# Norm factors spread by a transpose, three layer-norm tiles added up ahead by GpSimd, and rope's sine products moved to the vector engine

## The chip, the cores and the metric

The kernel runs on one core of a Trainium2 chip. The metric is the device time of one execution in microseconds (us), the median of three runs.

## What is computed

Two decoder layers over 1024 positions and 1024 channels, everything in float32. Of the reference, what bears on the change:

```python
h = _rmsnorm(x, mix_norm_gain[layer])
q, k, v, conv_in = jnp.split(h @ w_in[layer], ...)
q = _rope(_rmsnorm(q, q_norm_gain[layer]), cos, sin)      # per head of 64: x1*cos - x2*sin, x2*cos + x1*sin
k = _rope(_rmsnorm(k, k_norm_gain[layer]), cos, sin)
attn = _dilated_attention(q, k, v)
a, g = jnp.split(conv_in, 2, axis=-1)
u = _causal_dwconv(a * jax.nn.sigmoid(g), ...)            # 31 taps, 512 channels
u = jax.nn.silu(_layernorm(u, ...))                       # over the 512 channels
x = x + jnp.concatenate([attn, u], -1) @ w_out[layer]
h = _rmsnorm(x, ffn_norm_gain[layer])
x = x + (silu(gate) * val of a 3-tap conv of h @ w_up) @ w_down[layer]
```

## The kernel before

Activations stand transposed in SBUF: channels on the 128 partitions, the 1024 positions along a row, so a tile is 128x1024. TensorE is written here as PE, the vector engine as DVE, ScalarE as ACT, GpSimd as POOL, the queue of the sync engine as SP.

**Order of the work.** Each engine has its program written out by hand, and semaphores that only count up tie them together; `at(l, per_layer, base, step, i)` is the count that a wait asks for in layer `l`, pass `i`. A layer has these stages:

1. Input projection: 20 units of 48 matmuls (8 k-tiles, 3 products of split operands, 2 halves of 512 columns), two PSUM buffers `mm`. They come in four groups of four: value and gate of one of four conv channel tiles (`CT = 4`), then the two halves of one of four query or key groups (`QKG = 4`); then four units for v. The loop `Fori(0, QKG - 1)` has the next group's units beside the last group's norm and rope.
2. Attention: 2 turns (`TURNS`) of 4 heads times 8 query blocks, 32 steps a turn. DVE's mask operation (L1085) reads PSUM `mm` and the table `logcount`, and between steps DVE runs the last conv taps (L1118), 22 a turn.
3. The sum over channels for the layer norm (L573), output projection `out_unit`, 8 units; then the FFN in 11 groups.

**What DVE does in the projection.** Beside each unit it splits the weights (`lo`, L931), multiplies the result by the norm factor (`scaled`, L943) and runs conv taps (`taps`, L964), each `y = u_pad * tap + y` over a whole tile with a drain behind it. In each group it also runs `qk_norm` (L998, L999) and `qk_rope`: o1 = ta*cos (L1006), o2 = tg*cos (L1007), a drain, then the wait for `qk_sin`, then o1 - m2 and o2 + m4 (L1012, L1013). m2 = tg*sin and m4 = ta*sin are POOL's (L1281, L1282), which start when DVE's drain at L1001 has counted `qk_normed` up. In the last group `read_v` sits between the wait and L1012: it reads a unit of v out of PSUM (L943). ACT then copies o1 and o2 into m2 and m4, SP stores them and loads the heads for attention from there.

**Spreading a factor.** The sum of squares of 128 positions is one number for each position. `sums` makes it (L421), POOL raises it to -1/2 (`rsqrt`, L1257), ACT repeats it 128 times along a row (`widen`), and `spread` (L430) turns it so that the factor lies along the positions, eight 128x128 blocks by the identity into `stat_b`. There are seven a layer: one for the first norm, four for query and key, one for the layer norm, one for the second norm.

**Layer norm mean.** The sum over 512 channels of y is made on PE by a matmul of `ones` with each of the four tiles of y, for two halves: eight matmuls (L573), behind attention's last operation. DVE subtracts the mean (L1144). POOL's other adds are `add_squares` (L1264), the squares of query and key (L1271) and the squares of the layer norm (L1285). The tiles ahead of a y tile are ready when its taps are: `conv_y` counts them, the second near the end of attention's first turn, the third in the middle of the second, the fourth near its end.

Of the kernel before, what the change touches and what calls it, by code (L numbers as in the profile page):

```python
# [26 lines left out]
ALU = mybir.AluOpType  # L27
# [3 lines left out]
P = 128  # L31
D_MODEL = 1024
SEQ = 1024
# [17 lines left out]
CT = CONV_CH // P  # L51
# [3 lines left out]
QKG = 2 * HEADS // HPT  # L55
# [19 lines left out]
QK_STORES = 16 * 4 * HPT * QKG  # L75
# [49 lines left out]
def trunk(nc, xT, positions, weights, gains, qk_gains, conv_par, ffn_par, inv_freq, mask, outT):  # L125
    ctx = ExitStack()
    with ctx:
        def sb(name, shape, dt=F32, to=ctx):
            return to.enter_context(nc.sbuf_tensor(name, shape, dt))

        def sem(name):
            return ctx.enter_context(nc.semaphore(name))
# [9 lines left out]
        sin = sb("sin", [P, SEQ])  # L142
        logcount = sb("logcount", [P, SEQ])
        rinv = sb("rinv", [P, SEQ])
        ident = sb("ident", [P, P])
        ones = sb("ones", [P, P])
# [14 lines left out]
        y = sb("y", [P, CT, SEQ], to=mixer)  # L161
        u_pad = sb("u_pad", [P, CT, TAPS - 1 + SEQ], to=mixer)
# [3 lines left out]
        m2 = sb("m2", [P, SEQ], to=proj); m4 = sb("m4", [P, SEQ], to=proj)  # L166
        o1 = sb("o1", [P, SEQ], to=proj); o2 = sb("o2", [P, SEQ], to=proj)
        tg = sb("tg", [P, SEQ], to=proj); ta = sb("ta", [P, SEQ], to=proj)
        sa = sb("sa", [P, SEQ], to=proj); sb_ = sb("sb_", [P, SEQ], to=proj)
        v_raw = (o1, ta, tg, ta)  # L170
        proj.close()
        attn = ExitStack()

# [24 lines left out]
        stat_b, stat_s = aux  # L198
# [28 lines left out]
        gate_pre = sem("gate_pre"); gate_sig = sem("gate_sig")  # L227
        conv_u = sem("conv_u"); conv_first = sem("conv_first"); conv_y = sem("conv_y")
        qk_copied = sem("qk_copied"); qk_sqsum = sem("qk_sqsum")
        qk_normed = sem("qk_normed"); qk_sin = sem("qk_sin"); qk_roped = sem("qk_roped")  # L230
        qk_hi = sem("qk_hi"); qk_lo = sem("qk_lo")
        qk_stored = sem("qk_stored")
        v_ready = sem("v_ready"); v_turn_full = sem("v_turn_full"); v_turned = sem("v_turned")
# [20 lines left out]
        def at(l, per_layer, base, step=0, i=0):  # L254

            return l * per_layer + i * step + base
# [12 lines left out]
        def plain(eng):  # L269


            eng.sem_inc(waits_passed, 1)
# [104 lines left out]
        def _(pe):  # L377
# [3 lines left out]
            for acc, src in ((mm[0], o1), (mm[1], o2)):  # L381
                for c in range(HPT):
                    last = pe.matmul(acc[:, c * quarter:(c + 1) * quarter], ta[:, c * P:(c + 1) * P],
                                     src[:, 0:quarter], start=True, stop=True)
# [15 lines left out]
            with pe.Fori(0, DEPTH) as l:  # L400
# [24 lines left out]
                def spread(wide, s0, b0, step=0, i=0):  # L425

                    pe.wait_ge(widened, at(l, SMALL, s0 + 1, step, i))
                    pe.wait_ge(statb_read, at(l, STAT_B, b0 + 1, step, i))
                    for b in range(TB):
                        last = pe.matmul(stat_b[:, b * P:(b + 1) * P], wide[:, b * P:(b + 1) * P], ident[:],  # L430
                                         start=True, stop=True)
                    last.then_inc(statb_full, 1)

                def norm_sums(squares, norm, s0):
# [8 lines left out]
                pe.wait_ge(down_read, at(l, DOWN, 2))  # L443
                norm_sums(squares1, 0, 0)
                unit(1, 1, 1, 1, midway=lambda: spread(sb_, 0, 0))
                unit(0, 0, U_QK, U_QK)
                unit(1, 1, U_QK + 1, U_QK + 1)
# [11 lines left out]
                sums((sa[:],), headsum[:], HPT, QKG)  # L459
                unit(1, 1, U_V + 1, U_V + 1)  # L460
                spread(sb_, QKG, QKG)

                def turn_v(t):
# [101 lines left out]


                pe.wait_ge(conv_y, at(l, CT, CT))
                for half in range(2):
                    cols = slice(half * BANK, (half + 1) * BANK)

                    pe.wait_ge(pt_read[half], at(l, TURNS * PT_TURN // 2, TURNS * PT_TURN // 2 + 1))
                    for c in range(CT):
                        last = pe.matmul(stat_b[:, cols], ones[:], y[:, c, cols], start=c == 0, stop=c == CT - 1)  # L573
                last.then_inc(statb_full, 1)
                pe.wait_ge(o_split, at(l, 2 * PAIRS, 2 * PAIRS))
                out_unit(0, 0)
# [302 lines left out]
        def _(dve):  # L879
# [22 lines left out]
            for dst, shift in ((o1[:, 0:quarter], 0.0), (o2[:, 0:quarter], 0.25)):  # L902
# [7 lines left out]
                src = ang  # L910
                for part in reduction_parts():
                    dve.scalar_tensor_tensor(dst, turns, -part, src, ALU.mult, ALU.add)
                    dve.drain()
                    src = dst
# [12 lines left out]
            with dve.Fori(0, DEPTH) as l:  # L927
# [68 lines left out]
                def qk_norm(i):  # L996
                    dve.wait_ge(statb_full, at(l, STAT_B, 2, 1, i))
                    dve.scalar_tensor_tensor(ta[:], ta[:], qkg[:, l * QKG + i, 0:1], stat_b[:], ALU.mult, ALU.mult)  # L998
                    dve.scalar_tensor_tensor(tg[:], tg[:], qkg[:, l * QKG + i, 1:2], stat_b[:], ALU.mult,  # L999
                                             ALU.mult).then_inc(statb_read, 1)  # L1000
                    dve.drain().then_inc(qk_normed, 1)  # L1001

                def qk_rope(i, read_v=None):

                    dve.wait_ge(qk_stored, at(l, QK_STORES, 16, QK_STORES // QKG, i))
                    dve.tensor_tensor(o1[:], ta[:], cos[:], ALU.mult)  # L1006
                    dve.tensor_tensor(o2[:], tg[:], cos[:], ALU.mult)  # L1007
                    dve.drain()  # L1008
                    dve.wait_ge(qk_sin, at(l, 2 * QKG, 2, 2, i))
                    if read_v:  # L1010
                        read_v()
                    dve.tensor_tensor(o1[:], o1[:], m2[:], ALU.subtract).then_inc(qk_roped, 1)  # L1012
                    dve.tensor_tensor(o2[:], o2[:], m4[:], ALU.add).then_inc(qk_roped, 1)  # L1013
                    dve.drain()
# [40 lines left out]
                lo(0, U_V + 2)  # L1055
                taps(CT - 1, TAPS_NEXT[4:])
                qk_norm(QKG - 1)
                lo(1, U_V + 3)

# [174 lines left out]
        @block.gpsimd  # L1234
        def _(pool):
            pool.memset(ident[:], 0.0)
            pool.drain()
            pool.affine_select(out=ident[:], in_=ident[:], compare_op=ALU.not_equal, fill=1.0, base=0,
                               pattern=[[-1, P]], channel_multiplier=1)
            pool.drain().then_inc(consts_ready, 1)  # L1240

            pool.tensor_copy(ta[:, 0:HPT * P].rearrange("p (c h f) -> p c h f", c=HPT, h=HPT),
                             ident[:].rearrange("p (c f) -> p c f", c=HPT).unsqueeze(2).broadcast_to(
                                 [P, HPT, HPT, HALF]))
            pool.drain().then_inc(consts_ready, 1)
            for t in range(KT):
                pool.wait_ge(x_loaded[t], 16)
                pool.sem_inc(x_updated, 1)
            pool.wait_ge(consts_ready, 3)
            pool.wait_ge(rope_ready, 2)  # L1250
            plain(pool)

            with pool.Fori(0, DEPTH) as l:
                def rsqrt(width, s0, step=0, i=0):

                    pool.wait_ge(small_read, at(l, SMALL, s0 + 2, step, i))
                    pool.tensor_tensor(small[:, 0:width], small[:, 0:width], neghalf[:].broadcast_to([P, width]),  # L1257
                                       ALU.pow).then_inc(pow_done, 1)

                def add_squares(squares, norm):  # L1260

                    for t in range(1, KT // 2):
                        pool.wait_ge(x_sq, at(l, 2 * KT, norm * KT + t + 1))
                        pool.tensor_tensor(squares[0], squares[0], squares[t], ALU.add).then_inc(sq_added, 1)  # L1264
                        pool.drain()

                add_squares(squares1, 0)
                rsqrt(TB, 0)
                with pool.Fori(0, QKG) as i:
                    pool.wait_ge(qk_copied, at(l, 2 * QKG, 2, 2, i))  # L1270
                    pool.tensor_tensor(sa[:], sa[:], sb_[:], ALU.add).then_inc(qk_sqsum, 1)  # L1271

                    pool.wait_ge(small_read, at(l, SMALL, S_QK + 2, 1, i))
                    by_head = small[:].rearrange("p (b h) -> p b h", h=HPT)
                    pool.tensor_tensor(by_head, by_head, eps_ms[:].unsqueeze(2).broadcast_to([P, TB, HPT]), ALU.add)
                    pool.drain()
                    rsqrt(TB * HPT, S_QK, 1, i)
                    pool.wait_ge(qk_normed, at(l, QKG, 1, 1, i))

                    pool.wait_ge(qk_stored, at(l, QK_STORES, 16, QK_STORES // QKG, i))  # L1280
                    pool.tensor_tensor(m2[:], tg[:], sin[:], ALU.mult).then_inc(qk_sin, 1)  # L1281
                    pool.tensor_tensor(m4[:], ta[:], sin[:], ALU.mult).then_inc(qk_sin, 1)  # L1282
                for c in range(1, CT):
                    pool.wait_ge(ln_sq, at(l, CT, c + 1))
                    pool.tensor_tensor(tg[:], sa[:] if c == 1 else tg[:], (sa, sb_)[c % 2][:], ALU.add  # L1285
                                       ).then_inc(ln_added, 1)
                    pool.drain()
                rsqrt(TB, S_LN)
                add_squares(squares2, 1)
                rsqrt(TB, S_NORM2)  # L1290
# [85 lines left out]
```

## Time and profile before

| what | value |
|---|---|
| median of 3 runs | 2617.43 us (2616.72 to 2618.36) |
| span of the profiled execution | 2619.3 us |
| PE busy | 2491.9 us (95%) |
| DVE busy | 1601.5 us (61%) |
| ACT busy | 792.5 us (30%) |
| POOL busy | 188.1 us (7%) |
| chain that ended last | PE 72%, DVE 13%, DVEq 7% of the span |

The profile of one execution gives each instruction's start and duration in us from the start of the span. The span is all that it says of its own time; it is 1.9 us above the median of the runs. DVEq is DVE's instruction queue, mostly a drain that waits for the operation ahead of it. A PE matmul in float32 is recorded as two instructions, one in the split form or a transpose as one. Matmuls overlap, so the distance between starts is what one costs.

### The profile page before, as it was taken

Reading aid. Unit: us, or ns where it says so; the run is one execution under the profiler, and the core shown is the slowest. Engines: PE = TensorE matmul, PEld = TensorE weight load, DVE = VectorE, ACT = ScalarE, POOL = GpSimd, SP = SyncE. Lnnn points to the kernel's source line nnn. Section 1 sums busy time; section 2 is a strip of 40 time slices with the busy share of each in tenths; the row PEclk is TensorE's granted clock in tenths of the full one; section 3 lists DMA queues with packets and bytes.
Section 4 is the critical chain, followed back from the end, with each engine's and each line's share of the span. In section 5 each row is a group of like instructions: output and inputs, shape, how many; then the busy total and the mean of one; then the engine's idle time right before and its main releaser. Section 6 shows DMA issues by size and latency. Waiting matters only on the chain.

```text
span 2619.3 us, 33211 instructions
## 1 busy us (share of the span) xinstructions
PE 2491.9 (95%) x11824; PEld 2064.4 (79%) x11824; DVE 1601.5 (61%) x1490; ACT 792.5 (30%) x1037; POOL 188.1 (7%) x71
## 2 busy tenths in 40 slices
PE   6999889999999999999989997889999999999998
PEld 5878678778888888888778776787788888888887
DVE  5788867454555555555548897664465555555555
ACT  4222355333222222222332224553332222222221
POOL 1223100110000000000002330001100000000000
PEclk8999889999999999999989998999999999999999
DMA  3232631011111111111002226300111111111111
GB/s 120 63 90 72 177 89 48 24 41 49 49 49 48 48 48 48 48 48 48 32 34 73 80 80 185 89 24 32 41 49 48 48 48 48 48 48 48 48 48 72
DMA packets 46379, 159.29 MB, mean 61 GB/s; under 512 B 7392, under 2 KB 7776, under 8 KB 46304
## 3 DMA queue, kind: packets, MB, share of 16 engines
q1 hardware_dynamic: 45152, 154.12, 18.7%
q10 hardware_dynamic: 1152, 4.19, 0.4%
q8 instruction: 44, 0.72, 0.1%
q14 instruction: 31, 0.25, 0.0%
HBM read 133.12 MB, written 25.17 MB: 60 GB/s over the span
## 4 chain that ended last, share of the span: by engine, by line
PE 72%; DVE 13%; DVEq 7%; issue 3%; ACT 2%; DMA 1%; SPq 1%; ACTq 0%
PE mm L397 44%; PE aux L397 19%; DVE y L964 7%; PE aux L536 4%; PE aux L520 2%; DVEq L966 2%; PE mm L500 2%; DVE y L1118 1%; DVEq L1008 1%; DVEq L1120 1%; PE aux L421 1%; PE aux L573 1%; DVE o L1006 1%; DVEq L1001 1%; ACT x_hi L670 1%
## 5 line engine op out<-in xcount | busy, mean ns | idle before, releaser
L397 PE MATMUL mm<-x_hi,w_hi 128*128 128x512 f32 x2304 | 727.3, 397 | 34.7 <-DVE x_lo L937 17.0
L397 PE MATMUL mm<-x_lo,w_hi 128*128 128x512 f32 x2304 | 718.3, 393 | 0.0
L397 PE MATMUL mm<-x_hi,w_lo 128*128 128x512 f32 x2304 | 718.3, 393 | 0.0
L397 PEld LDWEIGHTS mm<-x_hi,w_hi 128*128 128x128 f32 x2304 | 434.9, 190 | 132.4 <-DVE x_lo L937 19.4
L397 PEld LDWEIGHTS mm<-x_lo,w_hi 128*128 128x128 f32 x2304 | 437.4, 190 | 96.1
L397 PEld LDWEIGHTS mm<-x_hi,w_lo 128*128 128x128 f32 x2304 | 436.6, 189 | 93.9
L647 ACT ACTIVATE w_hi<-w_raw 128x1024 fp32r<-128x1024 f32 x188 | 197.2, 1058 | 767.7 <-PE mm L397 576.2
L1133 DVE TENSOR_TENSOR x<-x,aux 128x1024 f32<-128x1024 f32 x176 | 214.8, 1220 | 136.4 <-PE aux L397 126.9
L931 DVE TENSOR_TENSOR w_lo<-w_raw,w_hi 128x1024 fp32r<-128x1024 f32 x188 | 228.2, 1222 | 38.3 <-ACT w_hi L647 25.1
L964 DVE SCALAR_TENSOR_TENSOR y<-u_pad,cpar,y (+1 forms) x152 | 210.8, 1387 | 26.2 <-issue 26.2
L943 DVE TENSOR_TENSOR uv<-mm,rinv 128x1024 f32<-128x1024 f32 x44 | 53.9, 1225 | 220.8 <-PE mm L397 220.5
L943 DVE TENSOR_TENSOR ug<-mm,rinv 128x1024 f32<-128x1024 f32 x44 | 53.9, 1225 | 179.3 <-PE mm L397 152.5
L1085 DVE CUSTOM_DVE_ANT_0 sc<-mm,logcount 128x128 f32<-128x128 f32 (+7 forms) x128 | 95.9, 756 | 86.3 <-PE mm L500 47.8
L536 PE MATMUL aux<-x_lo,pT 128*128 128x64 f32 x1152 | 148.7, 277 | 0.0
L536 PEld LDWEIGHTS aux<-x_lo,pT 128*128 128x128 f32 x1152 | 145.2, 200 | 1.2
L397 PE MATMUL aux<-h_hi_even,w_hi 128*128 128x512 f32 x384 | 120.9, 396 | 5.8 <-DVE w_lo L931 5.8
L397 PE MATMUL aux<-h_lo_even,w_hi 128*128 128x512 f32 x384 | 121.6, 398 | 0.0
L397 PE MATMUL aux<-h_hi_even,w_lo 128*128 128x512 f32 x384 | 120.3, 394 | 0.0
L772 ACT ACTIVATE sc<-sc,small 128x128 f32<-128x128 f32 (+7 forms) x128 | 99.4, 777 | 68.1 <-DVE small L1085 67.9
L1118 DVE SCALAR_TENSOR_TENSOR y<-u_pad,cpar,y x88 | 112.7, 1281 | 0.3
L520 PE MATMUL aux<-ident,sc 128*128 128x128 f32 x576 | 91.2, 286 | 20.5 <-DVE x_lo L1096 9.2
L783 ACT ACTIVATE pT<-aux 128x512 f32<-128x512 f32 (+1 forms) x192 | 86.5, 484 | 54.8 <-PE aux L520 54.4
(152 smaller groups left out, 2493.9 us busy)
## 6 DMA issues: line engine op xcount, KB each, us to landing
w_raw<-weights SPq DMA_DIRECT2D x188, 512.0 KB, 3.3
qk_scratch<-m SPq DMA_DIRECT2D x64, 128.0 KB, 2.1
qk_scratch<-o SPq DMA_DIRECT2D x64, 128.0 KB, 2.1
x_hi<-qk_scratch SPq DMA_DIRECT2D x32, 256.0 KB, 6.0
x<-xT ACTq DMA_DIRECT2D x8, 512.0 KB, 11.2
q_st<-qk_scratch SPq DMA_DIRECT2D x8, 512.0 KB, 3.5
k_hh<-qk_scratch SPq DMA_DIRECT2D x16, 256.0 KB, 5.7
k_ll<-qk_scratch SPq DMA_DIRECT2D x16, 256.0 KB, 6.1
```

What stands on the lines that cost most here:

```text
L397: last = pe.matmul(acc[:, cols], a, b[:, cols], start=start and n == 0, stop=stop and n == 2)
L520: last = pe.transpose(bank[:, c * P:(c + 1) * P], block_, ident[:])
L536: last = pe.matmul(out, pT[n % 2][:, kb, :], vp[b][:, kb, hh * HEAD_DIM:(hh + 1) * HEAD_DIM], start=kb == 0, stop=kb == qb)
L647: act.activation(w_hi[slot][:], w_raw[raw][:], ACT.Copy).then_inc(w_hi_ready, 1)
L772: act.activation(s, s, ACT.Exp, bias=neg_max[:, n % 4:n % 4 + 1], scale=-1.0, accum_out=row_sum[:, h % 2, qb:qb + 1]).then_inc(exp_done, 1)
L783: act.activation(pT[which % 2][:, a:z, :], bank[:, 0:(z - a) * P].rearrange("p (k q) -> p k q", q=P), ACT.Copy).then_inc(pt_read[f % 2], 1)
L931: dve.tensor_tensor(w_lo[slot][:], w_raw[base % 2][:], w_hi[slot][:].bitcast(F32), ALU.subtract).then_inc(weights_split, 1)
L943: dve.tensor_tensor(dst, mm[buf][:], rinv[:], ALU.mult).then_inc(mm_read, 1)
L964: dve.scalar_tensor_tensor(y[:, c, :], u_pad[:, c, j:j + SEQ], cpar[:, l * CT + c, j:j + 1], y[:, c, :], ALU.mult, ALU.add)
L1085: dve.tensor_tensor_reduce(sc[n % 3][:, 0:keys], mm[n % 2][:, 0:keys], logcount[:, SEQ - keys:SEQ], -SCALE, 3e38, ALU.add, ALU.min, neg_ma ...
L1118: dve.scalar_tensor_tensor(y[:, ch, :], u_pad[:, ch, j:j + SEQ], cpar[:, l * CT + ch, j:j + 1], y[:, ch, :], ALU.mult, ALU.add)
L1133: dve.tensor_tensor(t, t, buf[:], ALU.add).then_inc(read, 1)
```

## The change

Three edits. `spread` issues a transpose for each block in place of a matmul by the identity. GpSimd adds tile 0 and 1 of y, then tile 2, into `y_sum`, which lies in the first tile of `u_pad` (its taps are done by then); L573's loop then runs over `y_sum` and tile 3, and PE waits for `y_summed`. The two sine products go from POOL to DVE, between the cosine products, and the semaphores `qk_normed` and `qk_sin` go.

```diff
+        y_sum = u_pad[:, 0, 0:SEQ]
...
-                        last = pe.matmul(stat_b[:, b * P:(b + 1) * P], wide[:, b * P:(b + 1) * P], ident[:],
-                                         start=True, stop=True)
+                        last = pe.transpose(stat_b[:, b * P:(b + 1) * P], wide[:, b * P:(b + 1) * P], ident[:])
...
                 pe.wait_ge(conv_y, at(l, CT, CT))
+                pe.wait_ge(y_summed, at(l, CT - 2, CT - 2))
...
-                    for c in range(CT):
-                        last = pe.matmul(stat_b[:, cols], ones[:], y[:, c, cols], start=c == 0, stop=c == CT - 1)
+                    for src in (y_sum, y[:, CT - 1, :]):
+                        last = pe.matmul(stat_b[:, cols], ones[:], src[:, cols], start=src is y_sum,
+                                         stop=src is not y_sum)
...
-                    dve.drain().then_inc(qk_normed, 1)
+                    dve.drain()
...
                     dve.tensor_tensor(o1[:], ta[:], cos[:], ALU.mult)
+                    dve.tensor_tensor(m2[:], tg[:], sin[:], ALU.mult)
                     dve.tensor_tensor(o2[:], tg[:], cos[:], ALU.mult)
+                    dve.tensor_tensor(m4[:], ta[:], sin[:], ALU.mult)
                     dve.drain()
-                    dve.wait_ge(qk_sin, at(l, 2 * QKG, 2, 2, i))
...
                     rsqrt(TB * HPT, S_QK, 1, i)
-                    pool.wait_ge(qk_normed, at(l, QKG, 1, 1, i))
-
-                    pool.wait_ge(qk_stored, at(l, QK_STORES, 16, QK_STORES // QKG, i))
-                    pool.tensor_tensor(m2[:], tg[:], sin[:], ALU.mult).then_inc(qk_sin, 1)
-                    pool.tensor_tensor(m4[:], ta[:], sin[:], ALU.mult).then_inc(qk_sin, 1)
+                for c in range(1, CT - 1):
+                    pool.wait_ge(conv_y, at(l, CT, c + 1))
+                    pool.tensor_tensor(y_sum, y[:, 0, :] if c == 1 else y_sum, y[:, c, :], ALU.add
+                                       ).then_inc(y_summed, 1)
+                    pool.drain()
```

## Rows read from the trace of the kernel before

**Rows 1.** The profile's page: busy time, and the chain that ended last.

```profile
PE 2491.9 (95%) x11824; PEld 2064.4 (79%) x11824; DVE 1601.5 (61%) x1490; ACT 792.5 (30%) x1037; POOL 188.1 (7%) x71
...
PE 72%; DVE 13%; DVEq 7%; issue 3%; ACT 2%; DMA 1%; SPq 1%; ACTq 0%
PE mm L397 44%; PE aux L397 19%; DVE y L964 7%; PE aux L536 4%; PE aux L520 2%; DVEq L966 2%; PE mm L500 2%; DVE y L1118 1%; DVEq L1008 1%; DVEq L1120 1%; PE aux L421 1%; PE aux L573 1%; DVE o L1006 1%; DVEq L1001 1%; ACT x_hi L670 1%
```

**Rows 2.** DVE in order of time, first group: start, duration, operation, [idle before].

```profile
114.87 2.88 DVE L1006 TENSOR_TENSOR o<-ta,cos 128x1024 f32<-128x1024 f32 x1 [0.46 <-issue]
117.67 3.41 DVE L1007 TENSOR_TENSOR o<-tg,cos 128x1024 f32<-128x1024 f32 x1
121.31 1.23 DVE L1012 TENSOR_TENSOR o<-o,m 128x1024 f32<-128x1024 f32 x1 [0.23 <-issue]
122.45 1.22 DVE L1013 TENSOR_TENSOR o<-o,m 128x1024 f32<-128x1024 f32 x1
```

**Rows 3.** POOL in order of time, first layer's projection.

```profile
113.24 3.43 POOL L1281 TENSOR_TENSOR m<-tg,sin 128x1024 f32<-128x1024 f32 x1 [9.82 <-DVEq L1001]
...
133.18 2.39 POOL L1271 TENSOR_TENSOR sa<-sa,sb_ 128x1024 f32<-128x1024 f32 x1 [13.18 <-ACT sb_ L704]
```

**Rows 4.** DVE in order of time, second and fourth group.

```profile
133.41 3.25 DVE L964 SCALAR_TENSOR_TENSOR y<-u_pad,cpar,y  x1 [0.20 <-issue]
...
165.24 3.11 DVE L1006 TENSOR_TENSOR o<-ta,cos 128x1024 f32<-128x1024 f32 x1 [0.23 <-issue]
...
171.91 1.23 DVE L1012 TENSOR_TENSOR o<-o,m 128x1024 f32<-128x1024 f32 x1 [0.23 <-issue]
...
263.61 3.42 DVE L1006 TENSOR_TENSOR o<-ta,cos 128x1024 f32<-128x1024 f32 x1
...
270.60 1.22 DVE L943 TENSOR_TENSOR ta<-mm,rinv 128x1024 f32<-128x1024 f32 x1 [0.23 <-issue]
```

**Rows 5.** PE in order of time, first layer's projection.

```profile
181.26 1.22 PE L397 MATMUL mm<-x_hi,w_hi 128*128 128x512 f32 x2 [3.00 <-DVE w_lo L931]
...
232.08 1.21 PE L397 MATMUL mm<-x_hi,w_hi 128*128 128x512 f32 x2 [1.99 <-DVE w_lo L931]
...
257.37 1.95 PE L430 MATMUL aux<-ident,sb_ 128*128 128x128 f32 x16
259.15 1.04 PE L472 MATMUL aux<-ident,o 128*128 128x128 f32 x8
259.94 0.71 PE L397 MATMUL mm<-x_hi,w_hi 128*128 128x512 f32 x2
271.92 1.09 PE L472 MATMUL aux<-ident,ta 128*128 128x128 f32 x8 [0.82 <-DVEq L1049]
```

**Rows 6.** The chain that ended last, in order of time: start, duration, what.

```profile
282.49 2.73 DMA qk_scratch<-o
...
508.46 1.80 PE aux L430 x16
```

**Rows 7.** PE in order of time, behind the first layer's attention.

```profile
470.24 9.20 PE L573 MATMUL aux<-y,ones 128*128 128x512 f32 x16 [0.77 <-DVE x_lo L1096]
478.88 1.03 PE L397 MATMUL mm<-x_hi,w_hi 128*128 128x512 f32 x2
```

**Rows 8.** Windows of 1 us: busy (x instructions) by engine, PE's granted clock, DMA.

```profile
473.00:474.00 1.00, 1.00 (x3) 0.48 (x2) 0.00 (x0) 0.00 (x0) 0.00 (x0) 0.50 0.00 0
474.00:475.00 1.00, 1.00 (x4) 0.35 (x3) 0.00 (x0) 0.00 (x0) 0.00 (x0) 0.78 0.00 0
```

**Rows 9.** DVE in order of time, second turn of attention.

```profile
414.16 1.28 DVE L1118 SCALAR_TENSOR_TENSOR y<-u_pad,cpar,y  x1
...
418.04 1.28 DVE L1118 SCALAR_TENSOR_TENSOR y<-u_pad,cpar,y  x1
```

**Rows 10.** POOL and DVE in order of time, at the layer norm.

```profile
489.20 2.40 POOL L1285 TENSOR_TENSOR tg<-tg,sb_ 128x1024 f32<-128x1024 f32 x1 [0.22 <-issue]
...
490.38 1.22 DVE L1133 TENSOR_TENSOR x<-x,mm 128x1024 f32<-128x1024 f32 x1 [4.22 <-PE mm L397]
```

More of the change, by code:

```diff
@@ L229, in trunk @@
         qk_copied = sem("qk_copied"); qk_sqsum = sem("qk_sqsum")
-        qk_normed = sem("qk_normed"); qk_sin = sem("qk_sin"); qk_roped = sem("qk_roped")
+        qk_roped = sem("qk_roped")
+        y_summed = sem("y_summed")
         qk_hi = sem("qk_hi"); qk_lo = sem("qk_lo")
```

## The prediction

> **What bounds the kernel now.** I read the page first [rows 1]. PE is busy 95% of the span and POOL 7%, but the chain that ended last is what prices an edit. It runs on PE for 72% and on DVE and its drains for 20%, and DVE's part names the lines of the projection: the conv taps (L964), the cosine products (L1006) and a stall in DVE's queue at L1008, which is the drain behind them. So the rope is on the path, and so are the layer-norm sum (L573) and the matmuls by the identity (L430).
>
> Then the timelines of the projection, engine by engine. DVE never stands idle for more than its own drains there: [rows 2] show it going straight on. PE does wait, for DVE's weight split, 3.00 us in the third group and 1.99 us behind it, and 0.82 us for v [rows 5]. So DVE sets the pace of the four groups, but with little to spare: those three waits, 5.81 us a layer, are PE's whole slack. The second layer repeats the first to 0.1 us at these places.
>
> The reader should then see why two cosine products take 2.88 and 3.41 us [rows 2] where the subtraction L1012, with the same shape and also both operands in SBUF, takes 1.23. POOL runs its first sine product from 113.24 to 116.67 [rows 3]. L1006 ends at 114.87 + 2.88 = 117.75, 1.08 us behind that. The conv tap at 133.41 [rows 4] takes 3.25 us, and another POOL add begins at 133.18 and ends at 135.57 [rows 3]; the tap ends at 136.66, 1.09 us behind. A tap otherwise takes 1.28 [rows 9]. The two engines shut each other out while both read two operands from SBUF, and DVE finishes one bare operation after POOL lets go. It does not hold where DVE takes one operand from PSUM: L1133 at 490.38 takes its 1.22 us in the middle of a POOL add from 489.20 to 491.60 that takes 2.40 [rows 10].
>
> **Rope.** From the start of L1006 to the first operation behind the wait DVE takes 121.31 - 114.87 = 6.44 us in the first group [rows 2], 171.91 - 165.24 = 6.67 in the second, the same again in the third, and 270.60 - 263.61 = 6.99 in the fourth [rows 4], where the fourth's successor is the reading of v. That is 26.77 us a layer. Afterwards there are four products and the same drain. With POOL silent I take each at the price of L1012 and L1013: the next starts 122.45 - 121.31 = 1.14 us later, the last lasts 1.23, the drain's gap is 0.23 [rows 2]. Four: 3 x 1.14 + 1.23 + 0.23 = 4.88 us. DVE so does twice the products in less time. The gain is 26.77 - 4 x 4.88 = 7.25 us a layer, 14.5 us in all, if DVE keeps the pace.
>
> What would take over? PE. Its slack is 5.81 us of waits, but after two of them its first matmul pair takes 1.2 us where 0.6 to 0.7 is usual (the last L397 row of [rows 5] takes 0.71), and four spreads a layer get shorter ahead of these waits (next part). That puts PE's own end of the projection about 5.8 + 4 x 0.9 = 9.4 us earlier, more than DVE's 7.25. The other hand-overs lie in order behind DVE: ACT copies o1, SP stores the quarters of query and key, one queue for all, the last store lands at 282.49 + 2.73 = 285.22 and attention's loads are issued only then [rows 6]. No DMA is added, and those on the path wait for DVE's results, so I let the whole 7.25 through to attention. Lower bound, if only PE's waits are to be had: 5.81 a layer, 11.6 in all.
>
> **Spread.** Eight matmuls by the identity are 16 instructions, and the next work starts 259.15 - 257.37 = 1.78 us later; eight transposes of v, with the same tile shape and the same identity, take 259.94 - 259.15 = 0.79 [rows 5]. Against a matmul as successor the first is about 1.7, so I take 0.9 for each spread. Only three of the seven a layer are on the path: the first norm's, the layer norm's (508.46, 1.80 us long [rows 6]) and the second norm's, each with ACT's and DVE's reading of the factor or PE's next unit right behind. The four of query and key are covered by DVE's taps and only give PE the slack above. 6 x 0.9 = 5.4 us. Bounds: nothing gained (0), and 6 x 0.99 = 5.9.
>
> By the Trainium skill, TensorE: Matmul & The Clock Gate, § Terms, the transpose mode is four times faster for float32; a spread would then fall from 1.78 to 0.45 us, six would give 8.0 us and the sum below would end at 2588.3. The same page in § Part 4: PE-mode transpose has about 275 ns for one transpose in a kernel, which laid end to end would be 2.2 us for eight, slower than now. Neither is what the distance between starts shows here, 0.10 us, and I stay with the row.
>
> **Layer-norm sum.** L573 has 16 instructions from 470.24, and the next unit starts at 478.88 [rows 7], 8.64 us. The granted clock is 0.50 (1.2 GHz) until into the 475th microsecond, whose mean is 0.78 [rows 8]; PE had been waiting for attention's last copies. At 0.78 the turn lies 0.44 us into that stretch, so 4.2 us ran at the low clock and 4.4 at the high one: 4.2 / 2 + 4.4 = 6.5 us of full-speed work, 0.41 us an instruction. Eight go. If the clock comes back at the same moment, the eight removed are those at full speed: 8 x 0.41 = 3.3 us a layer, 6.6 in all. The bounds: at the low clock throughout, 8 remaining cost 6.6 us and 2.0 is gained a layer (4.0 in all); all of the removed at the low clock, 6.6 a layer (13.2). I take 3.3, since PE's wait ahead is unchanged. DVE's subtraction and the layer norm's POOL adds shift together with PE.
>
> **GpSimd's two new adds a layer.** Each is 2.40 us like the one in [rows 10]. The first may start when the last tap of turn 1 is done; DVE has no further tap until the next turn. The second starts behind the tap of 414.16, so at about 415.7, and ends at about 418.1; the next tap is at 418.04 [rows 9]. Between them DVE runs only mask operations, whose one operand is in PSUM. By [rows 10] these go on. A tap that meets POOL's last 0.1 us costs nothing that can be seen. Both sums are there over 50 us before L573 asks. I take 0. Upper bound, if a mask operation is shut out after all: the whole 2.40 for each, 9.6 us for four. POOL's queue holds nothing else that is waited for then.
>
> **Sum.** 14.5 + 5.4 + 6.6 + 0 = 26.5 us. Against the profiled span 2619.3 this gives 2592.8; the median of the runs is 1.9 us below that span, so 2617.4 - 26.5 = 2590.9 us.
>
> **Rivals.**
> - *PE takes the pace in the projection.* For it: its waits are 5.81 us, less than DVE's 7.25 [rows 5]. Against it: the shorter spreads ahead of them. The gain there is 11.6 instead of 14.5: 2593.8 us. 12%.
> - *The transpose saves nothing* in a stream of matmuls, or costs in the change of mode what it saves. Against it: 0.79 us in just such a place. 5.4 us less: 2596.3 us. 6%.
> - *The new adds stop DVE in attention.* The chain passes through DVE there (L1118 in [rows 1]). Against it: [rows 10], which however is an add and not the mask operation. 9.6 us less: 2600.5 us. 5%.
> - *Slower: the cosine products are slow by themselves*, say through their tables, and POOL's presence is chance. Then four products take twice as long as two do now, 6.7 us more in each of the eight groups: +53.5, less 5.4 + 6.6 = 12.0, so 2617.4 + 41.5 = 2658.9 us. It decides once a product costs more than (6.69 + 12.0 / 8) / 4 = 2.05 us. Against it: the ends 1.08 and 1.09 us behind POOL's, and a tap slowed in the same way. 3%.
>
> My forecast has 72%; 2% are left for a mixture that comes out within 0.2% of before.
>
> **Range.** Low end: the clock returning early enough behind attention that some removed instructions are slow ones (up to 6.6 us more); I take nine tenths of it, 5.9, which gives 2585.0. High end: the PE rival and the transpose rival together, 2590.9 + 2.9 + 5.4 = 2599.2. Outside lie the last two rivals and the mixture, 10%, and what the clock may do beyond. Within 0.2% (5.2 us) of before is about what a measurement of this kernel can't tell from no change. All cases but the last rival and the mixture are faster by more: 95%; same 2%, slower 3%.
>
> **What the next profile would show.** L1006, L1007 and the two new products at 1.22 us, first product to L1012 4.9 us; no wait of DVE for POOL. PE's waits for L931 at 3.00 and 1.99 nearly gone. Spread to next start 0.8. L573 with 8 instructions in about 5.4 us, clock at half for about 4 of it. Mask operations of 1.09 us unchanged beside the new POOL adds, and attention as long as before. The prediction is wrong if DVE begins to wait for PE in the groups, if products stay above 2 us, if attention grows, or if PE's clock falls in places where it did not.

## The result, and the profile after

| kernel | median us | executions | ratio to before, 95% interval |
|---|---|---|---|
| before | 2617.07 | 4 | |
| changed | 2585.88 (2576.16 to 2591.88) | 4 | 0.9873 (0.9854 to 0.9892) |
| changed, measured again | 2585.87 (2581.06 to 2586.93) | 4 | 0.9867 (0.9848 to 0.9887) |

The kernel is 1.3% faster, 31 to 35 us, where 26.5 were forecast. The ratio puts it at 2584.2 us beside the 2617.4 that the prediction started from, 0.8 us under the low end of the range, 2585.0; the interval of the ratio, 2579.2 to 2589.2 us, takes that end in, and the bare median, 2585.88, lies above it. The direction and the three terms' mechanisms were right; 5 to 7 us were not in the sum. The executions of the changed kernel also spread over 16 us, with their mean granted clock: 2576.16 at 0.980, 2582.16 at 0.977, 2589.59 at 0.975, 2591.88 at 0.972.

The page of the changed kernel, busy time and chain, beside [rows 1]:

```profile
PE 2461.7 (95%) x11696; PEld 2040.7 (79%) x11696; DVE 1586.2 (61%) x1506; ACT 793.1 (31%) x1037; POOL 143.8 (6%) x59
...
PE 73%; DVE 13%; DVEq 6%; issue 3%; ACT 2%; DMA 1%; SPq 1%; ACTq 0%
PE mm L399 45%; PE aux L399 19%; DVE y L967 7%; PE aux L537 4%; PE aux L521 2%; DVEq L969 2%; PE mm L501 2%; DVE y L1122 1%; DVEq L1124 1%; PE aux L423 1%; DMA k_ll<-qk_scratch 1%; DVEq L1004 1%; ACT x_hi L673 1%; DVE w_lo L934 1%; DVEq L967 0%
```

DVE has 16 instructions more and 15.3 us less to do. The cosine products and the stall behind them have left the chain. DVE in the second group of the changed kernel, beside [rows 2, 4]:

```profile
163.66 1.23 DVE L1009 TENSOR_TENSOR o<-ta,cos 128x1024 f32<-128x1024 f32 x1 [0.22 <-issue]
164.80 1.22 DVE L1010 TENSOR_TENSOR m<-tg,sin 128x1024 f32<-128x1024 f32 x1
165.94 1.22 DVE L1011 TENSOR_TENSOR o<-tg,cos 128x1024 f32<-128x1024 f32 x1
167.07 1.22 DVE L1012 TENSOR_TENSOR m<-ta,sin 128x1024 f32<-128x1024 f32 x1
168.37 1.23 DVE L1016 TENSOR_TENSOR o<-o,m 128x1024 f32<-128x1024 f32 x1
```

Four products in 168.37 - 163.66 = 4.71 us, where two took 6.67. Next, the layer norm's sum on PE, beside [rows 7]: the first of its four pairs, the last, and the next unit.

```profile
458.92 1.12 PE L575 MATMUL aux<-u_pad,ones 128*128 128x512 f32 x2 [1.18 <-DVE x_lo L1100]
...
461.60 1.02 PE L575 MATMUL aux<-y,ones 128*128 128x512 f32 x2
462.06 1.03 PE L399 MATMUL mm<-x_hi,w_hi 128*128 128x512 f32 x2
...
491.48 1.03 PE L432 MATMUL aux<-ident,sb_ 128*128 128x128 f32 x8
492.27 0.71 PE L399 MATMUL mm<-x_hi,w_hi 128*128 128x512 f32 x2
```

The sum takes 3.14 us instead of 8.64, and the last two rows are a spread, 0.79 us to the next start. The new adds beside the mask operations of attention, POOL first, then DVE:

```profile
406.24 2.37 POOL L1284 TENSOR_TENSOR u_pad<-u_pad,y 128x1024 f32<-128x1024 f32 x1 [45.00 <-DVEq L1124]
```

```profile
406.57 1.09 DVE L1089 CUSTOM_DVE_ANT_0 sc<-mm,logcount 128x896 f32<-128x896 f32 x1 [0.44 <-PE mm L501]
407.58 0.08 DVE L1089 DVE_READ_ACCUMULATOR2_ANT small<- 128x1 f32 x1
407.58 1.22 DVE L1089 CUSTOM_DVE_ANT_0 sc<-mm,logcount 128x1024 f32<-128x1024 f32 x1
```

Neither is slowed. Where the surplus lies shows when both traces are cut at the same events. Windows of the kernel before, first layer: attention's first turn, its second turn, and the stretch from the layer norm's spread to the second norm's. Behind the length stand the busy times of PE, its weight loads, DVE, ACT and POOL, then PE's granted clock (0.50 is 1.2 GHz, 1.00 is 2.4 GHz), the DMA share and GB/s.

```profile
296.60:384.90 88.30, 77.16 (x546) 69.30 (x544) 56.75 (x98) 49.70 (x117) 0.00 (x0) 0.92 0.44 123
384.90:470.20 85.30, 75.74 (x540) 68.19 (x540) 56.05 (x97) 49.92 (x117) 0.00 (x0) 0.92 0.14 37
...
508.30:600.00 91.70, 87.12 (x386) 71.81 (x385) 49.00 (x40) 35.09 (x35) 10.15 (x4) 0.94 0.12 43
```

The same of the changed kernel, with the sum between the second and the third:

```profile
289.90:375.60 85.70, 75.03 (x546) 67.21 (x544) 56.75 (x98) 50.02 (x117) 2.38 (x1) 0.95 0.47 120
375.60:458.90 83.30, 72.41 (x540) 65.21 (x540) 56.06 (x97) 49.68 (x117) 2.37 (x1) 0.98 0.15 38
458.90:462.10 3.20, 3.18 (x9) 1.51 (x9) 0.69 (x1) 0.00 (x0) 0.00 (x0) 1.00 0.02 5
...
491.50:579.30 87.80, 83.11 (x377) 68.39 (x376) 48.99 (x40) 35.10 (x35) 10.16 (x4) 0.98 0.14 45
```

And of the changed kernel's second layer, the first turn, the second and the sum:

```profile
1561.70:1650.00 88.30, 77.34 (x546) 69.61 (x544) 56.74 (x98) 49.82 (x117) 2.38 (x1) 0.92 0.44 120
1650.00:1735.20 85.20, 75.66 (x540) 68.16 (x540) 56.05 (x97) 50.05 (x117) 2.37 (x1) 0.93 0.14 37
1735.20:1740.50 5.30, 5.28 (x8) 2.23 (x9) 0.69 (x1) 0.00 (x0) 0.00 (x0) 0.58 0.01 3
```

In the first layer the first turn takes 85.7 us at a clock of 0.95 where it took 88.3 at 0.92, the second 83.3 at 0.98 where it took 85.3 at 0.92, and the sum takes 3.2 us at full clock. In the second layer of the same execution, with the same code, the turns take 88.3 us at 0.92 and 85.2 at 0.93, and the sum 5.3 at 0.58. DVE and ACT do the same work to 0.4 us in all these turns. So what differs is PE's clock, not the change's work.

The whole stretch from attention's first mask operation to the second norm's spread shows it at once. First and second layer of the kernel before, then of the changed kernel, then of the changed kernel measured again (run e9_after_again):

```profile
296.60:600.00 303.40, 278.07 (x1623) 237.55 (x1622) 174.45 (x246) 142.21 (x277) 19.01 (x8) 0.93 0.21 62
1595.50:1898.10 302.60, 276.85 (x1623) 235.50 (x1622) 174.43 (x246) 142.02 (x277) 19.28 (x8) 0.94 0.21 60
```

```profile
289.90:579.30 289.40, 263.12 (x1606) 226.71 (x1605) 174.45 (x246) 142.29 (x277) 23.77 (x10) 0.97 0.23 63
1561.70:1859.40 297.70, 272.47 (x1607) 234.07 (x1606) 174.43 (x246) 142.46 (x277) 24.00 (x10) 0.94 0.22 62
```

```profile
287.70:585.70 298.00, 272.78 (x1607) 234.32 (x1606) 174.44 (x246) 142.39 (x277) 23.76 (x10) 0.94 0.22 62
1568.80:1862.10 293.30, 268.41 (x1606) 229.74 (x1606) 174.45 (x246) 142.42 (x277) 24.03 (x10) 0.95 0.22 63
```

The change has 4.3 us less to do there in each layer (3.4 in the sum, 0.9 in a spread). In the first pair of traces the stretch is 14.0 us shorter in the first layer and 4.9 in the second; the changed kernel alone has it at 289.4, 297.7, 298.0 and 293.3 us, the shorter the higher its clock.

### The profile page after: what moved, and what is told of

Same layout as the page of the kernel before. It is cut to its first block, busy times and chain, and to the rows that moved or that the text cites. A ratio compares the mean times of both kernels' runs of the same rounds, so it can differ in the third digit from the quotient of the medians.

```text
span 2580.4 us, 32949 instructions
## 1 busy us (share of the span) xinstructions
PE 2461.7 (95%) x11696; PEld 2040.7 (79%) x11696; DVE 1586.2 (61%) x1506; ACT 793.1 (31%) x1037; POOL 143.8 (6%) x59
## 4 chain that ended last, share of the span: by engine, by line
PE 73%; DVE 13%; DVEq 6%; issue 3%; ACT 2%; DMA 1%; SPq 1%; ACTq 0%
PE mm L399 45%; PE aux L399 19%; DVE y L967 7%; PE aux L537 4%; PE aux L521 2%; DVEq L969 2%; PE mm L501 2%; DVE y L1122 1%; DVEq L1124 1%; PE aux L423 1%; DMA k_ll<-qk_scratch 1%; DVEq L1004 1%; ACT x_hi L673 1%; DVE w_lo L934 1%; DVEq L967 0%
## 5 line engine op out<-in xcount | busy, mean ns | idle before, releaser
L399 PE MATMUL mm<-x_hi,w_hi 128*128 128x512 f32 x2304 | 725.3, 396 | 30.5 <-DVE x_lo L940 16.2
L399 PE MATMUL mm<-x_hi,w_lo 128*128 128x512 f32 x2304 | 718.3, 393 | 0.0
L399 PE MATMUL mm<-x_lo,w_hi 128*128 128x512 f32 x2304 | 717.7, 393 | 0.0
L399 PEld LDWEIGHTS mm<-x_hi,w_hi 128*128 128x128 f32 x2304 | 433.9, 190 | 128.4 <-DVE x_lo L940 18.9
L399 PEld LDWEIGHTS mm<-x_lo,w_hi 128*128 128x128 f32 x2304 | 436.8, 190 | 95.5
L399 PEld LDWEIGHTS mm<-x_hi,w_lo 128*128 128x128 f32 x2304 | 436.7, 190 | 93.7
L946 DVE TENSOR_TENSOR uv<-mm,rinv 128x1024 f32<-128x1024 f32 x44 | 53.9, 1225 | 220.9 <-PE mm L399 220.5
L946 DVE TENSOR_TENSOR ug<-mm,rinv 128x1024 f32<-128x1024 f32 x44 | 53.9, 1225 | 175.3 <-PE mm L399 152.5
L1089 DVE CUSTOM_DVE_ANT_0 sc<-mm,logcount 128x128 f32<-128x128 f32 (+7 forms) x128 | 96.0, 757 | 80.8 <-PE mm L501 42.3
L399 PE MATMUL aux<-h_hi_even,w_hi 128*128 128x512 f32 x384 | 120.9, 396 | 5.8 <-DVE w_lo L934 5.8
L399 PE MATMUL aux<-h_lo_even,w_hi 128*128 128x512 f32 x384 | 121.8, 399 | 0.0
L399 PE MATMUL aux<-h_hi_even,w_lo 128*128 128x512 f32 x384 | 120.3, 394 | 0.0
L786 ACT ACTIVATE pT<-aux 128x512 f32<-128x512 f32 (+1 forms) x192 | 86.4, 484 | 48.6 <-PE aux L521 48.0
```

The source lines that it names most:

```text
L399: last = pe.matmul(acc[:, cols], a, b[:, cols], start=start and n == 0, stop=stop and n == 2)
L786: act.activation(pT[which % 2][:, a:z, :], bank[:, 0:(z - a) * P].rearrange("p (k q) -> p k q", q=P), ACT.Copy).then_inc(pt_read[f % 2], 1)
L946: dve.tensor_tensor(dst, mm[buf][:], rinv[:], ALU.mult).then_inc(mm_read, 1)
L1089: dve.tensor_tensor_reduce(sc[n % 3][:, 0:keys], mm[n % 2][:, 0:keys], logcount[:, SEQ - keys:SEQ], -SCALE, 3e38, ALU.add, ALU.min, neg_ma ...
```

## The experiments

Each kernel ran beside the kernel before on one chip. A stage's length is the distance between two starts in the trace of its profiled execution: "projection" from the first spread to DVE's reading of the second unit of v into ta, "turn" from its first mask operation to the next turn's (or to the layer-norm sum). "Work" is the mean over executions of span times granted clock, 2545 to 2547 us for the kernel before. It leaves out what a low clock takes from PE, but it also leaves out half of each us in which PE idles at low clock and loses nothing, so it is a rough measure. By it the changed kernel has 25.5 us less than the kernel before (run e9_after_again), and 8 us of low clock go as well.

**One edit at a time.** *Rope alone*: the hunks of `qk_norm`, `qk_rope` and POOL's loop in the diff, nothing else.

> Only the sine products move to the vector engine. Theory A (the work saved is as forecast, and what the changed kernel gained beyond it is PE's granted clock): the eight stretches from L1006 to L1012 or to the reading of v shrink from 26.77 to about 19.5 us a layer, and the span times its mean granted clock falls by 14.5 us (12 to 17) from 2548.7; the median itself falls by 14.5 give or take 6, moving with the mean clock of each execution. Theory B (the surplus is the rope's: fewer PE stalls give back more than DVE's saving): the span times clock falls by 18 us or more. Theory C (PE takes the pace): 11.6 us or less.

2601.53 us, ratio 0.9936 (0.9923 to 0.9948): 17 us less. The projection went from 215.8 to 207.9 us in the first layer and from 215.7 to 207.9 in the second, 7.9 and 7.8. Work fell by only 11.4, which is below theory A's 12 to 17 and looks like theory C, but the stage decides: in the kernel before, PE's clock was at 0.50 for 3.4 us at the end of each of its two waits for DVE's weight split and behind it (from 180.9 and from 232.1 us), where DVE set the pace and the slower PE cost no time, and these went with the waits. PE's waits for L931 in the first layer fell to one of 1.0 us. The term is right, and 1.2 us larger than forecast.

*Spreads alone*: the hunk of `spread`.

> Only the spreads become transposes. Theory A: eight transposes take 0.8 us instead of 1.7, on the path three times a layer, 5.4 us less in the span times mean clock; the median within 6 us of that, by the clock. Theory D (transposes leave PE's clock lower): more time at the granted clock of 0.50 than the kernel before, and a time that is the same or longer.

2603.83 us, ratio 0.9939 (0.9925 to 0.9952): 16 us less, three times the 5.4 forecast. Work fell by 6.1. The rest goes with the clock: the product of span and one minus clock has a mean of 60.3 us against 70.1 for the kernel before in the same comparison. The rope stretches and PE's order are as before; the projection is 0.9 us shorter. Neither theory had foreseen a surplus of 10 us. The padded kernel below is there for it.

*Layer-norm sum alone*: `y_sum`, POOL's two adds, PE's loop over two tiles.

> Only the layer-norm sum is made from the tile that GpSimd added up and the fourth tile. Theory A: L573's part goes from 16 to 8 instructions, 6.6 us less in the span times mean clock (8 x 0.41 a layer), attention as long as before but for its clock. Theory E (the new adds shut DVE out in attention): a mask operation beside them over 2 us instead of 1.1, and 6.6 less up to 9.6, so -6.6 to +3 us.

2613.88 us, ratio 0.9976 (0.9967 to 0.9986): 6.3 us less, work 7.2 less. In the first layer the low clock ends at the same moment as before, 474.4 us, and the sum takes 5.2 us instead of 8.6.

*The adds alone*, with the sum still over four tiles:

```diff
+                pe.wait_ge(y_summed, at(l, CT - 2, CT - 2))
...
                     for c in range(CT):
                         last = pe.matmul(stat_b[:, cols], ones[:], y[:, c, cols], start=c == 0, stop=c == CT - 1)
```

> GpSimd makes the two adds a layer and PE waits for them, but the sum is still made from the four tiles (the adds' result is not used). Theory A: 0 us, within 1.5, in the span times mean clock, so a difference of this run from the kernel before is the clock's alone. Theory E: up to 9.6 us slower.

2618.28 us, ratio 0.9997 (0.9987 to 1.0008). The four adds cost nothing; the prediction's third rival, in which they stop DVE (theory E), is out.

**Is the surplus the clock?** Matmuls that nobody reads, in the kernel before and in the changed one:

```diff
                 pe.wait_ge(v_turned, at(l, PAIRS, PAIRS))
+                pe.wait_ge(mm_read, at(l, MM, M_SCORE + 1))
+                for n in range(10):
+                    pe.matmul(mm[0][:, 0:BANK], ident[:], cos[:, 0:BANK], start=True, stop=True)
...
+                        if n < STEPS and n % TB < 3:
+                            hh = n // TB % 2
+                            pe.wait_ge(o_read, at(l, HEADS, n // TB + 1, TURN_HEADS, i))
+                            pe.matmul(stat_s[:, hh * BANK:(hh + 1) * BANK], ident[:], cos[:, 0:BANK],
+                                      start=True, stop=True)
```

> The kernel before, with matmuls whose results nobody reads put where PE stands idle: ten of 512 columns ahead of attention's first scores, one in each of the first three steps of every head. Theory A (what the changed kernel gained beyond its work terms is PE's granted clock in and behind attention): less time at 0.50 in attention than the 27 us of its two turns in the kernel before, and turns at their short values, 85.5 and 83.5 us, unless the fillers themselves come to stand on the path. Theory B (the clock is a side effect): the turns stay at 88 and 85 or grow by the fillers' time.

> The changed kernel with the same fillers. Theory A: its distance to the kernel before with fillers is the work alone, 28 us (25 to 31): 15.8 rope, 5.4 spreads, 6.8 layer-norm sum. Theory B (the surplus belongs to the change): 33 us or more.

2647.50 us, ratio 1.0110 (1.0092 to 1.0128), and 2619.99 us, ratio 1.0008 (0.9997 to 1.0018). The fillers stand on the path: both turns of the first layer of each, as a window:

```profile
302.20:488.50 186.30, 165.48 (x1135) 139.04 (x1133) 112.78 (x195) 99.11 (x234) 0.00 (x0) 0.99 0.26 67
```

```profile
290.50:481.10 190.60, 170.05 (x1134) 143.14 (x1132) 112.81 (x195) 99.14 (x234) 4.75 (x2) 0.96 0.25 65
```

The clock is up, 0.99 and 0.96 instead of 0.92, and attention is 13 us longer than without fillers in the kernel before and 22 in the changed one, so the forecast that the turns would come to their short values was wrong, and as a remedy this is none. As a comparison it serves: the two kernels' mean span times one minus clock is the same 42.3 us, and at that equal mean clock they lie 27.5 us apart by the medians, 26.7 by the ratios (1.0110 - 1.0008 = 0.0102). That is near the work of the change, and not the 33 us of the bare pair. The clock is equal in the mean only, though: in the two profiled executions the stretch from attention to the second norm takes 313.9 us at 0.98 in the kernel before and 315.8 at 0.96 in the changed one, and what the changed one loses there it has back in the FFN (745.3 us against 751.2 behind the first layer's stretch). So the pair supports the sum of the terms, and would not prove it alone.

**Transposes, but no shorter spread.** One matmul ahead of each spread's transposes:

```diff
+                    pe.matmul(stat_b[:, 0:BANK], ident[:], cos[:, 0:BANK], start=True, stop=True)
                     for b in range(TB):
                         last = pe.transpose(stat_b[:, b * P:(b + 1) * P], wide[:, b * P:(b + 1) * P], ident[:])
```

> Spreads as transposes, each with one matmul of 512 columns ahead of it, which makes a spread as long as before (1.6 to 1.7 us). Theory A (the transposes alone gained 10 us more than their 5.4 because all that follows lies elsewhere in time and the clock falls elsewhere): with the length the surplus goes too, 2619 give or take 4 us. Theory D (transposes themselves keep the clock up): still 8 us or more below the kernel before.

2613.52 us, ratio 0.9983 (0.9971 to 0.9995), 4.5 us less than before by the ratio, between the two theories and outside both of their bounds. The padded spread takes 1.65 us to the next start, as before (1.70). Of the 16 us of the transposes alone, some 11 went when the length came back. About 4 stayed, and the forecast of either theory missed them; by the rough measure work is 2.6 us less, and the mean clock is 0.9739 against 0.9730. The most that this shows is that most of the surplus hangs on where things lie in time.

**The other two edits without the rope.**

> The changed kernel with the rope's edit undone: transposes and the shorter layer-norm sum. Theory A: 15.8 us (13 to 19) above the changed kernel in work, so 2597 to 2603 at the changed kernel's clock, and 12.2 below the kernel before in the span times mean clock. Theory B (gains don't add up, since PE becomes the bound in the projection only with all three): less than 12 us above the changed kernel.

2601.65 us, ratio 0.9930 (0.9913 to 0.9947); the changed kernel's two ratios, 0.9867 and 0.9873, are 16.5 and 14.9 us below. In the stages the rope's edit is worth 8.3 and 8.4 us here (projections of 214.9 and 215.0 against 206.6). So it is worth about the same with the others as alone (17), and theory B is out.

**Again, and with POOL back.** The changed kernel was measured again, and beside it ran one in which POOL makes its products as well and DVE waits for them:

```diff
+                    dve.wait_ge(qk_sin, at(l, 2 * QKG, 2, 2, i))
...
+                    pool.wait_ge(qk_normed, at(l, QKG, 1, 1, i))
+                    pool.tensor_tensor(sb_[:], tg[:], sin[:], ALU.mult).then_inc(qk_sin, 1)
+                    pool.drain()
+                    pool.tensor_tensor(sb_[:], ta[:], sin[:], ALU.mult).then_inc(qk_sin, 1)
+                    pool.drain()
```

> The changed kernel once more, in more rounds and beside the other two. Theory A: 28 us of work less than the kernel before and some 5 of clock, so 2581 to 2591 us, single executions spread by over 10 us in step with their mean clock.

> The changed kernel, but GpSimd makes the sine products as well, into a tile nobody reads, and DVE waits for them as before. Theory A (the two engines shut each other out): two POOL operations of 2.4 us alternate with DVE's four, the stretch from L1009 to L1016 grows from 4.71 to 9 us or a little more, and the time by 8 x 4.5 = 36 us. Theory F (the cosine products were slow by their own, or the wait was what cost): products stay at 1.2 us and the stretch ends with POOL's second product, 6.8 us, 17 us in all.

2585.87 us for the first, as in the table above. The second: 2621.16 us, ratio 1.0004 (0.9988 to 1.0019), 35.3 us above the changed kernel by the medians, 36 forecast. POOL and DVE in its second group:

```profile
165.97 2.39 POOL L1285 TENSOR_TENSOR sb_<-tg,sin 128x1024 f32<-128x1024 f32 x1 [14.21 <-DVEq L1005]
168.52 3.18 POOL L1287 TENSOR_TENSOR sb_<-ta,sin 128x1024 f32<-128x1024 f32 x1 [0.16 <-issue]
```

```profile
166.06 3.38 DVE L985 TENSOR_TENSOR u_pad<-u_pad,o 128x1024 f32 x1 [0.22 <-issue]
169.67 3.11 DVE L1010 TENSOR_TENSOR o<-ta,cos 128x1024 f32<-128x1024 f32 x1 [0.23 <-issue]
172.71 1.21 DVE L1011 TENSOR_TENSOR m<-tg,sin 128x1024 f32<-128x1024 f32 x1
```

Each POOL operation holds up exactly one DVE operation, by about 2 us, which ends 1.08 us behind it, and which one is a matter of when: here the first lands on the product with the gate (L985) and not on a cosine product, so the stretch itself grew to 6.75 us only, while the projection grew from 206.6 to 224.2 us, 4.4 a group. DVE did not stand at its wait for `qk_sin`. Theory F, in which the wait is the cost, is out. The Trainium skill, SBUF — State Buffer, § Who interferes with whom, says that a DVE instruction with two inputs in SBUF contends with a GpSimd instruction that reads SBUF, and that one with at most one input there, outside the 2-port perf modes, doesn't. The traces agree on both: 3.38 us for two inputs here, 1.09 us unchanged for the mask operation of the changed kernel above.

**Further on the same road.** One POOL add in each group still meets a conv tap. First without it, PE summing both tiles of squares:

```diff
-                    sums((sa[:],), headsum[:], HPT, S_QK, 1, i)
+                    sums((sa[:], sb_[:]), headsum[:], HPT, S_QK, 1, i)
```

> The changed kernel without GpSimd's add of the squares of query and key (L1271 before); PE sums both tiles, 16 more instructions for 4 columns, 1.7 us a group. Theory A: the one conv tap a group that takes 3.1 to 3.3 us goes back to 1.28, 1.9 us a group on DVE, but PE gains 1.7 us of work and has little to spare, so between 0 and 12 us faster than the changed kernel; I expect 6. Theory G (PE is already the bound in the projection): 5 us slower or more.

2606.36 us, ratio 0.9947 (0.9928 to 0.9966), 20 us slower than the changed kernel. Theory G held and theory A fell: PE is busy through the whole projection of the first layer,

```profile
54.70:273.30 218.60, 218.60 (x1005) 183.24 (x1004) 166.07 (x137) 56.24 (x58) 25.50 (x8) 0.95 0.25 75
```

and at the narrow matmuls its clock falls. PE is busy 15.1 us longer than in the changed kernel's projection in the first layer (218.6 against 203.5) and 10.2 in the second (213.7); the narrow matmuls have 1.8 us a group of that at full clock, 7.2 a layer, and the low clock the rest. PE in the second group, where a pair of L399 usually starts every 0.45 us:

```profile
146.43 0.57 PE L423 MATMUL aux<-headsum,sa 128*128 128x4 f32 x2
146.85 0.57 PE L423 MATMUL aux<-headsum,sb_ 128*128 128x4 f32 x2
147.28 1.20 PE L399 MATMUL mm<-x_hi,w_hi 128*128 128x512 f32 x2
148.28 1.05 PE L399 MATMUL mm<-x_lo,w_hi 128*128 128x512 f32 x2
149.13 1.05 PE L399 MATMUL mm<-x_hi,w_lo 128*128 128x512 f32 x2
```

DVE waits for PE there, 16.6 us in four waits of L946 and 5.9 in one of L1001. Then the same add on DVE:

```diff
                     dve.wait_ge(qk_copied, at(l, 2 * QKG, mbase // 2 + 1, 2, i))
                     dve.sem_inc(mm_read, 1)
+                    dve.tensor_tensor(sa[:], sa[:], sb_[:], ALU.add).then_inc(qk_sqsum, 1)
                     lo(1, mbase + 3, 4, i)
```

> The changed kernel with GpSimd's add of the squares of query and key moved to DVE, ahead of its second weight split of a group. Theory A: DVE pays 1.14 us for the add and saves the 1.85 us by which a conv tap waits for GpSimd, 0.7 us a group, 5.7 us in eight groups, so the projection goes from 206.6 to 203.8 us a layer and the time to 2580 give or take 4, by the clock. PE's remaining waits for DVE are 3.2 us in the first layer's groups, so 4.6 us may be all. Theory G (PE is the bound already): the projection stays at 206.6.

2573.52 us (2571.08 to 2579.55), ratio 0.9827 (0.9808 to 0.9845), faster than both kernels. DVE in the second group of the changed kernel, beside POOL's add, and of this one:

```profile
133.40 3.13 DVE L967 SCALAR_TENSOR_TENSOR y<-u_pad,cpar,y  x1 [0.20 <-issue]
```

```profile
135.25 1.29 DVE L967 SCALAR_TENSOR_TENSOR y<-u_pad,cpar,y  x1 [0.20 <-issue]
136.80 1.23 DVE L997 TENSOR_TENSOR sa<-sa,sb_ 128x1024 f32<-128x1024 f32 x1 [0.27 <-issue]
137.94 1.22 DVE L934 TENSOR_TENSOR w_lo<-w_raw,w_hi 128x1024 fp32r<-128x1024 f32 x1
```

The tap of 3.13 us is gone, the projection takes 203.4 us in both layers, 3.2 less, 2.8 forecast. That is 6.4 us of work; the ratios lie 10 us apart (0.9827 and 0.9867), and the mean clock is 0.9778 against 0.9755.

## Why the prediction was right, and where it was not

**Rope, right.** The two engines shut each other out; four products on DVE alone are cheaper than two beside POOL. Forecast 14.5 us, measured 15.7 in the stages (rope alone) and 16.4 in the changed kernel (18.2 less two spreads of 0.9). The working took 1.14 us to the next start for three of the products, and 1.23 and a gap of 0.23 for the last, 4.88; it is 4.71, since the drain behind it adds nearly nothing. What was forecast as 7.25 a layer passed through to attention, as argued: PE's waits did not become the limit.

**Spread, right in its work.** 0.8 us forecast and 0.79 measured, three a layer on the path, 6.1 us of work against 5.4. By the Trainium skill, TensorE: Matmul & The Clock Gate, § Terms, it would have been a quarter of 1.70; it is a little under half.

**Layer-norm sum, right in its work.** At one clock 8.6 against 5.2 us; at full clock 6.6 (rope alone, 463.3 to 469.9) against 3.1: 3.4 to 3.5 a layer, 3.3 forecast. Its upper bound was wrong, 6.6 us a layer: with all of the low clock gone 8 instructions of 0.41 us are left, so some 8.64 - 3.28 = 5.4 us is the most that the first layer can give, and it gave 5.5. **The new adds, right**: nothing.

These measured terms make 15.7 + 5.4 + 6.9 = 28.0 us, where the sum had 26.5; with the rope as measured in the changed kernel, 28.7. The kernels with fillers lie 26.7 to 27.5 apart. So 1.5 to 2.2 of the missing 5 to 7 us are the sizes of the terms, the rope's above all.

**The step that failed is the clock.** The prediction took it as given: "If the clock comes back at the same moment", "I take 3.3, since PE's wait ahead is unchanged", and in its last part "attention as long as before". It let the clock move in one place, the layer-norm sum, and only for the low end of the range. But all that stood behind a shortened stage lay elsewhere in time, and PE's falls to half speed came elsewhere. In the first pair of traces this gave, beyond the work, 2.6 us in the first layer's first turn, 2.0 in its second, 2.2 in the sum (5.5 less 3.3) and 3.0 before the second norm (3.9 less the spread's 0.9). In the second layer the same stages gave -1.5, 1.3, 1.0 and nothing. Another 1.6 us over both layers came from the way to attention (26.0 and 28.4 us before, 27.4 and 25.5 after), which the prediction also took as given; in the second layer the load of k_ll that attention waits for took 10.32 us before and 8.71 after, and no run shows this to be the change's. When the same kernel was measured again, the surplus lay elsewhere: the first layer's stretch took 298.0 us, where it had been 289.4 and where the work alone would give 303.4 - 4.3 = 299.1, and the second layer's took 293.3, where the work alone would give 298.3. So the gain of any one trace is in part luck. Over the executions the mean clock went from 0.9730 or so to 0.9757, and with it went what the sizes leave of the surplus, 3 to 5 us.

That most of this is the clock's is shown by stretches of equal code, with equal work on DVE and ACT, that are the shorter the higher PE's clock, and supported by the pair with fillers. Why a spread 0.9 us shorter gives 10 us of it, and why the padded one keeps 4, stays open: the traces show where the clock falls, not why there.

Of the range: its low end gave the clock 5.9 us in the two layer-norm sums, somewhat more than they hold (8.6 and 9.6 us long before, less 3.28 and the forecast 3.3 each: 5.1 in all), and nothing in the other stages. The kernel before already showed what they can do, for its two layers run the same code: 88.3 and 86.8 us for the first turn, 85.3 and 86.4 for the second, 91.7 and 90.3 before the second norm. The prediction compared the layers in the projection only, where they agree. Differences of 1.1 to 1.5 us in each of six stages (four turns, two norms) would be some 8 us if all fell one way: an estimate from rows that lay open, and the low end had no room for it. Later traces went further, 83.3 to 88.6 us for the second turn without fillers. The result lay 0.8 us outside, less than its own scatter.

## What to carry to other kernels

Two engines that read SBUF pairwise at the same time may serve each other by turns: look for an operation that ends a fixed time behind another engine's, and price a move by what it takes alone. A gain on PE's path has a second part that the sum of durations doesn't hold, where PE's clock will fall afterwards; give it room in the range in each stage with idle PE time, and compare spans with their mean clocks beside them. When one engine's stall is taken away, ask at once how much slack the next has: the same POOL add was worth 10 us moved to DVE and cost 20 moved to PE.

## What the runs showed of the hardware

Sixteen more narrow matmuls (4 columns) a group took 1.8 us themselves, and in six of the eight groups PE's clock fell to half in them or just behind them, for 3.4 us in one group and 6.8 in five; wide pairs took 0.85 us there instead of 0.45, although PE had not stood idle. The kernels of this study also have no single time: executions of one program differed by up to 19 us (2610.8 to 2629.4 for the kernel with both products), the longer ones in the main at the lower mean clock. The two traces of the changed kernel, 2580.4 and 2583.3 us long, have DVE busy for 1586.2 us in both and ACT for 793.1 and 793.3.
